# Four key weight tiles of the second block taken feature tile by feature tile, with two halves split before the normalisation root

## Chip, cores and metric

The kernel runs on one core of one Trainium2 chip, as one launch. The metric is the device time of that core in microseconds; of several runs the median counts. The engines are named as in the profile: PE is TensorE's matrix multiply and PEld its weight loads, DVE is VectorE, ACT is ScalarE, POOL is GpSimd, SP issues the weight stream's DMAs.

## What is computed

Three transformer-like blocks run over 256 tokens with 1024 features. The first two (`DEPTH = 2`) also carry 256 context tokens, so that their keys and values span 512 columns. The change lies at the seam between the first and the second block. There the reference does, for tokens `x` and context `xc`:

```python
x_new = x + gt[:, None] * rms_norm(out, norm_post[l])
...
h = rms_norm(x, norm_pre[l]) * (1.0 + sc[:, None]) + sh[:, None]
hc = rms_norm(xc, norm_pre[l]) * (1.0 + scc) + shc
z = h @ w_in[l]
zc = hc @ (w_in[l][:, :COL_Q] if last else w_in[l])
kc = qk_heads(zc[..., COL_K:COL_V])
...
k = apply_rope(qk_heads(z[..., COL_K:COL_V]), cos, sin)
```

The 512 key columns of `w_in` make four weight tiles, the 512 query columns four, the 512 value columns four. Keys are needed for all 512 columns (tokens and context), queries in the second block for the 256 tokens alone.

## The kernel before

Activations are kept feature-major: 1024 features are 8 feature tiles (`KT = 8`) of 128 partitions, with the 512 tokens along the free axis. Weights arrive as one stream of tiles of 128 x 1024 numbers (512 KB each), in the order in which they are used. Each tile `t` passes through four stations:

- SP loads it into one of `RAW = 4` slots; it waits until the slot's earlier tile has been split (`tile_lo`, t - 4).
- ACT writes the high half, rounded to fp32r (`act_hi`, L999, name `whi`). It waits for the landing and for `used`, t - 4: PE must be through with the tile whose `whi` slot is overwritten, since there are `SPLIT = 4` slots.
- DVE writes the low half, raw minus high (`dve_lo`, L1435, name `wlo`).
- PE multiplies it with three matmuls for each feature tile (`three`, L376 to L378: low by high, high by low, high by high), accumulating over the 8 feature tiles in one of four PSUM banks `gemm_bank`. The last matmul marks `used`, and ACT evacuates the bank (L1023 for key and query tiles).

Every engine works through a program written by hand, in order; a wait holds all that stands behind it. ACT has the high halves three tiles ahead of the tile it evacuates and DVE the low halves two tiles ahead.

Around the seam (`l = 1`) the program is as follows. PE sums the squares of the new `x`, turns two adaLN rows into columns (L519) and multiplies four adaLN tiles (L447). ACT splits the high halves of key tiles 0, 1 and 2, copies the adaLN row (L1018) and takes the root of the mean square (`act_root`, L990). DVE splits the low halves of key tiles 0 and 1, copies the turned adaLN values (L1550), finishes the modulation vectors (L1789, L1790), takes the reciprocal of the root (`dve_rstd`, L1427), and then makes the normalised input for each feature tile (`dve_h`): a sum on DVE (L1807, name `tmp`), the high half on ACT (L1233, name `hhi`), the low half on DVE (L1818, name `hlo`). PE's first key tile waits for each feature tile in turn (`begun`), the other three do not need to.

After `dve_h` DVE splits four tiles (key tiles 2 and 3, query tiles 0 and 1), then works out the argument of the third block's rotary cosine (`dve_trig`, L1635 to L1564, a long chain of small operations each of which waits for the one before), splits query tile 2, works out the argument of the sine, and then splits query tile 3 and three value tiles. ACT answers each argument with a `Sin` (L1266), ahead of which an ACT_TABLE_LOAD stands. DVE's second argument waits for ACT's first `Sin`, since both use one buffer; DVE's splitting of query tile 3 waits for the second.

Of the kernel before, what the change touches and what calls it, by code (L numbers as in the profile page):

```python
# [14 lines left out]
P = 128  # L15
D = 1024
KT = D // P
# [8 lines left out]
SPLIT = 4  # L26
# [20 lines left out]
          [("rope", P, ALL), ("perm1", P, P), ("inv_freq", P, 1), ("head_gain", P, 15), ("causal", P, P), ("cmp_add", P, 2 * NCMP),  # L47
           ("cmp_any", P, 2), ("perm2", P, P), ("head_sum", P, 14 * 32), ("block_mean", P, P), ("pe_k", P, 16), ("pe_v", P, 16),
           ("g_mix", P, 8), ("g_ffn", P, 8), ("g_ple", P, 8)]


def pi_parts():
# [152 lines left out]
class Kernel:  # L205
# [396 lines left out]
    def pe_front(self):  # L602
# [21 lines left out]
        self.pe_tiles(4)  # L624
        self.pe_turn(0, 3)

    def pe_first(self):

        self.pe_tiles(1)
        self.pe_taps(0)  # L630
        self.pe_tiles(4)
        self.pe_tap_norm(0)
        self.pe_tiles(2)
        self.pe_spec(0)
        self.pe_tiles(1)
# [148 lines left out]
    def pe_block1(self, l):  # L784
        n = TOK if l else ALL
        if l == 0:
            self.pe_first()
        self.pe_tiles(9 if l else 1)
        for a, b in ROPE:
            self.pe_rope(l, a, b)  # L790
            self.pe_tiles(1)
        if l == 0:
            self.pe_tiles(1)
        self.pe_attention(l)
        self.pe_conv(l)
        self.pe_tiles(4 if l else 1)
        self.pe_gmlp(l)
        self.pe_tiles(8 + (28 if l else 36))
        for o in range(KT):
            self.pe_tiles(1)  # L800
            if o:
                self.pe_sum(("out", l), o - 1, n)
            if l == 0 and o in (0, 2):
                self.pe_hidden(1, o // 2)
            if l == 0 and o == 4:
                self.pe_taps(1)
        if l == 0:
            self.pe.wait_ge(*self.at("taps", 1))
        self.pe_sum(("out", l), KT - 1, n)
        if l == 0:  # L810
            self.pe_tap_norm(1)
            self.pe_tiles(4)
            self.pe_spec(1)
        self.pe.wait_ge(*self.at("rstd", ("out", l)))
        for k in range(KT):
            self.pe_sum(("res", l), k, n)
        if l == 0:
            self.pe_turn(1, 4)
            self.pe_tiles(4)
            self.pe_turn(1, 5)  # L820
# [435 lines left out]
    def act_block1(self, l):  # L1256
        act, n = self.act, TOK if l else ALL
        if l:
            self.act_root(("res", 0), ALL)
        act.wait_ge(*self.at("mod", l))  # L1260
        self.act_h(l)
        if l:
            self.act_tiles(4)
            for i in range(2):
                act.wait_ge(*self.at("trig_arg", i))
                act.activation((self.cos, self.sin)[i], self.tmp[:, 1, 0:TOK], ACT.Sin).then_inc(*self.mark("act_filter", "trig", i))  # L1266
                if i == 0:
                    self.act_tiles(1)
            self.act_tiles(7)
        else:  # L1270
            self.act_first()
            self.act_tiles(4)
        if l == 0:
            self.act_tiles(1)
        self.act_attention(l)
        self.act_conv(l)
        self.act_tiles(4 if l else 1)
        self.act_gmlp(l)
        act.wait_ge(*self.at("gm_y", l, 1 if l else 3))
        self.act_tiles(8 + (28 if l else 36))  # L1280
        act.wait_ge(*self.at("evac", self.tiles[self.act_done - 1].use))
        self.act_merged(l, KT - 1, n)
        for o in range(KT):
            self.act_tiles(1)
            if l == 0 and o in (1, 3):
                self.act_hidden(1, o // 2)
            if l == 0 and o == 6:
                self.act_tap_sq(1)
        self.act_root(("out", l), n)
        if l == 0:  # L1290
            self.act_tap_root(1)
            self.act_tiles(4)
        for k in range(KT):
            act.wait_ge(*self.at("x_new", l, k))
            self.act_sq(("res", l), k, n, self.x[:, k, 0:n]).then_inc(*self.mark("act_sq", "sq", ("res", l), k))
            if l == 0 and k >= 3 and k < 7:
                self.act_kern(1, k - 3)
        if l == 0:
            self.act_tiles(4)
# [536 lines left out]
    def dve_block1(self, l):  # L1836
        v, n = self.dve, TOK if l else ALL
        if l:
            self.dve_rstd(("res", 0), ALL)
        self.dve_h(l)  # L1840
        if l:
            self.dve_tiles(4)
            self.dve_trig()
            self.dve_tiles(4)
        else:
            self.dve_first()
            self.dve_tiles(4)
        for a, b in ROPE:
            self.dve_rope(l, a, b)
            self.dve_tiles(1)  # L1850
        if l == 0:
            self.dve_tiles(1)
        self.dve_attention(l)
        self.dve_conv(l)
        self.dve_tiles(4 if l else 1)
        self.dve_gmlp(l)
        self.dve_tiles(8 + (28 if l else 36))
        self.dve_merged(l, KT - 1, n)
        for o in range(KT):
            self.dve_tiles(1)  # L1860
            if l == 0 and o in (0, 2):
                self.dve_hidden(1, o // 2)
            if l == 0 and o == 5:
                self.dve_taps(1)
                self.dve_tap_sd(1)
        if l == 0:
            self.dve_mod(1)
            self.dve_tap_add(1)
            self.dve_tiles(4)
        self.dve_rstd(("out", l), n)  # L1870
        if l == 0:
            self.dve_tap_rs(1)
        for k in range(KT):
            out = self.branch_out[:, k, 0:n]
            self.own(v.tensor_tensor(out, out, self.tmp[:, 2, 0:n], ALU.mult))
            v.tensor_tensor(self.x[:, k, 0:n], self.x[:, k, 0:n], out, ALU.add).then_inc(*self.mark("dve_x", "x_new", l, k))
        if l == 0:
            self.dve_turned(1, 4)
            self.dve_tiles(4)
            self.dve_turned(1, 5)  # L1880
            self.dve_mod_gate(1)
# [435 lines left out]
```

## Time and profile before

| what | value |
|---|---|
| median of 3 runs | 1585.3 us (1583.09 to 1588.12) |
| the profiled execution, its own time | 1588.17 us |
| its span in the profile | 1586.8 us |
| mean granted TensorE clock | 0.973 |
| PE busy | 1484.6 us, 94% of the span |
| DVE busy | 896.8 us, 57% |
| ACT busy | 675.2 us, 43% |
| the seam read here | 700 to 760 us of the span |

The profiled execution took 1.4 us more than its span, which is what lies outside of the instructions. It was 2.9 us slower than the median of the three timed runs, and equal to their highest. Times in the rows below are counted from the span's start. The busy share is an average over the whole kernel; the stretch of the change is read by itself.

### The profile page before, as it was taken

The numbers are of one execution on the slowest core, as the hardware profiler recorded it, in microseconds if no ns is written. First come the engines' busy times: TensorE is split into PE (matmuls) and PEld (weight loads), VectorE is DVE, ScalarE is ACT, GpSimd is POOL, SyncE is SP. The second block draws the span as 40 slices with busy tenths as digits, with TensorE's granted clock in tenths as the row PEclk, the third lists the DMA queues.
The fourth block names the chain that finished last, engine by engine and source line by source line (L and its number), as shares of the span: only waits on it lengthen the run. The fifth ranks groups of instructions, "written<-read, shape, count | busy, mean of one in ns | idle before, by whom it ended". The sixth has DMA issues, their size and how long they took to land. (4 is left out here: it accounts for less than half of the span.)

```text
span 1586.8 us, 22164 instructions
## 1 busy us (share of the span) xinstructions
PE 1484.6 (94%) x8986; PEld 1250.4 (79%) x8986; DVE 896.8 (57%) x1653; ACT 675.2 (43%) x1176; POOL 32.5 (2%) x42
## 2 busy tenths in 40 slices
PE   6799999987999999978989999988999999999998
PEld 2577667765888888736778889987878889999997
DVE  3525764654533434457576576656666547666546
ACT  3432544123322223444455354456556544544434
POOL 0000000000000000100000000010000001000000
PEclk9899999998999999999999999999999999999999
DMA  8521442124232322332323346544542215555552
GB/s 318 173 67 53 135 159 92 53 86 146 93 107 91 103 85 93 99 133 67 107 93 128 145 146 190 180 148 136 173 146 81 67 62 170 182 185 181 192 174 80
DMA packets 57847, 203.14 MB, mean 128 GB/s; under 512 B 6257, under 2 KB 9457, under 8 KB 57617
## 3 DMA queue, kind: packets, MB, share of 16 engines
q1 hardware_dynamic: 55568, 194.01, 37.0%
q0 software_dynamic: 1888, 7.12, 1.3%
q8 instruction: 71, 1.16, 0.3%
q10 hardware_dynamic: 288, 0.58, 0.1%
q14 instruction: 32, 0.25, 0.1%
HBM read 200.65 MB, written 1.05 MB: 127 GB/s over the span
## 5 line engine op out<-in xcount | busy, mean ns | idle before, releaser
L376 PE MATMUL gemm_bank<-hhi,wlo 128*128 128x256 f32 (+1 forms) x1264 | 415.5, 329 | 38.8 <-DVE wlo L1435 15.7
L1435 DVE TENSOR_TENSOR wlo<-raw,whi 128x1024 fp32r<-128x1024 f32 x316 | 381.0, 1219 | 75.7 <-ACT whi L999 71.7
L999 ACT ACTIVATE whi<-raw 128x1024 fp32r<-128x1024 f32 x316 | 332.0, 1052 | 189.3 <-PE gemm_bank L378 120.9
L377 PE MATMUL gemm_bank<-hlo,whi 128*128 128x256 f32 (+1 forms) x1264 | 399.0, 316 | 0.0
L378 PE MATMUL gemm_bank<-hhi,whi 128*128 128x256 f32 (+1 forms) x1264 | 398.2, 315 | 0.0
L376 PEld LDWEIGHTS gemm_bank<-hhi,wlo 128*128 128x128 f32 x1264 | 246.2, 195 | 67.3 <-issue 24.6
L378 PEld LDWEIGHTS gemm_bank<-hhi,whi 128*128 128x128 f32 x1264 | 246.5, 195 | 14.1
L377 PEld LDWEIGHTS gemm_bank<-hlo,whi 128*128 128x128 f32 x1264 | 247.2, 196 | 12.9 <-issue 0.7
L376 PE MATMUL misc_bank<-hhi,wlo 128*128 128x256 f32 (+1 forms) x496 | 160.7, 324 | 0.0
L377 PE MATMUL misc_bank<-hlo,whi 128*128 128x256 f32 (+1 forms) x496 | 160.7, 324 | 0.0
L378 PE MATMUL misc_bank<-hhi,whi 128*128 128x256 f32 (+1 forms) x496 | 160.7, 324 | 0.0
L376 PE MATMUL gemm_bank<-arena_r,wlo 128*128 128x256 f32 (+1 forms) x408 | 132.9, 326 | 0.6 <-issue 0.6
L378 PE MATMUL gemm_bank<-arena_r,whi 128*128 128x256 f32 (+1 forms) x408 | 132.5, 325 | 0.0
L377 PE MATMUL gemm_bank<-arena_r,whi 128*128 128x256 f32 (+1 forms) x408 | 132.5, 325 | 0.0
L376 PEld LDWEIGHTS misc_bank<-hhi,wlo 128*128 128x128 f32 x496 | 94.4, 190 | 7.5
L378 PEld LDWEIGHTS misc_bank<-hhi,whi 128*128 128x128 f32 x496 | 94.4, 190 | 7.5
L377 PEld LDWEIGHTS misc_bank<-hlo,whi 128*128 128x128 f32 x496 | 94.4, 190 | 7.4
L376 PEld LDWEIGHTS gemm_bank<-arena_r,wlo 128*128 128x128 f32 x408 | 77.6, 190 | 8.5 <-issue 2.3
L378 PEld LDWEIGHTS gemm_bank<-arena_r,whi 128*128 128x128 f32 x408 | 77.6, 190 | 6.3
L377 PEld LDWEIGHTS gemm_bank<-arena_r,whi 128*128 128x128 f32 x408 | 77.6, 190 | 6.1
L1470 DVE SCALAR_TENSOR_TENSOR tmp<-tmp,gemm_bank 128x512 f32<-128x512 f32 (+1 forms) x32 | 17.7, 555 | 104.1 <-ACT tmp L1060 104.1
L1060 ACT ACTIVATE tmp<-misc_bank 128x512 f32<-128x512 f32 (+1 forms) x40 | 20.5, 512 | 122.5 <-PE misc_bank L378 122.5
(334 smaller groups left out, 1942.4 us busy)
## 6 DMA issues: line engine op xcount, KB each, us to landing
raw<-in_stream SPq DMA_DIRECT2D x364, 512.0 KB, 3.5
const_b<-in_const_b POOLq DMA_DIRECT2D x1, 1100.0 KB, 8.7
x<-in_x SPq DMA_DIRECT2D x1, 1024.0 KB, 8.7
x<-in_ctx SPq DMA_DIRECT2D x1, 1024.0 KB, 11.0
y<-in_hy_decay POOLq DMA_DIRECT2D x2, 512.0 KB, 6.6
arena<-in_gm_ws POOLq DMA_DIRECT2D x2, 512.0 KB, 6.1
y<-in_hy_w POOLq DMA_DIRECT2D x2, 256.0 KB, 5.4
shared<-in_dft POOLq DMA_DIRECT2D x1, 512.0 KB, 4.1
```

What stands on the lines that cost most here:

```text
L376: mm(out, w_lo, r_hi, start=first, stop=False)
L377: mm(out, w_hi, r_lo, start=False, stop=False)
L378: return mm(out, w_hi, r_hi, start=False, stop=last)
L999: act.activation(self.whi[:, t % SPLIT, :], self.raw[:, t % RAW, :], ACT.Copy).then_inc(*self.mark("tile_hi", "tile_hi", t))
L1060: act.activation(self.tmp[:, e % 2, 0:n], self.M[e][:, 0:n], ACT.Tanh, scale=0.5).then_inc(*self.mark("act_sel", "sel_tanh", T.use))
L1435: dve.tensor_tensor(self.wlo[:, t % SPLIT, :], self.raw[:, t % RAW, :], self.whi[:, t % SPLIT, :].bitcast(F32), ALU.subtract).then_inc(*se ...
L1470: self.own(dve.scalar_tensor_tensor(th, th, 1.0, b[:, 0:n], ALU.add, ALU.mult))
```

## The change

Three things change, all in the second block, and no instruction is added or removed.

PE takes the four key tiles together (`pe_quad`, order in `QUAD`): (0, 1) means key tile 0, feature tile 1. Each of the four accumulates in its own bank. Up to feature tile 3 the tiles advance together, then tiles 0 and 1 in turns, then tile 2 and tile 3 to their ends. Key tiles 2 and 3 therefore need both their halves before PE begins with them, so ACT splits key tile 3 ahead of `act_root`, and DVE splits key tiles 2 and 3 ahead of `dve_rstd`. Behind `dve_h` as many splits are left out (`split=False`).

```diff
--- before.py
+++ after.py
@@ -47,6 +47,9 @@
           [("rope", P, ALL), ("perm1", P, P), ("inv_freq", P, 1), ("head_gain", P, 15), ("causal", P, P), ("cmp_add", P, 2 * NCMP),
            ("cmp_any", P, 2), ("perm2", P, P), ("head_sum", P, 14 * 32), ("block_mean", P, P), ("pe_k", P, 16), ("pe_v", P, 16),
            ("g_mix", P, 8), ("g_ffn", P, 8), ("g_ple", P, 8)]
+
+QUAD = [(0, 0), (0, 1), (1, 0), (1, 1), (0, 2), (1, 2), (2, 0), (2, 1), (2, 2), (0, 3), (1, 3), (2, 3), (3, 0), (3, 1), (3, 2), (3, 3)] + \
+       [(i, k) for k in range(4, KT) for i in (0, 1)] + [(i, k) for i in (2, 3) for k in range(4, KT)]
 
 
 def pi_parts():
@@ -624,6 +627,23 @@
         self.pe_tiles(4)
         self.pe_turn(0, 3)
 
+    def pe_quad(self):
+
+        pe, tiles, n = self.pe, self.tiles[self.pe_next:self.pe_next + 4], 0
+        for i, k in QUAD:
+            T = tiles[i]
+            s, c = T.t % SPLIT, slice(k * P, (k + 1) * P)
+            if k == 0:
+                pe.wait_ge(*self.at("tile_lo", T.t))
+                self.pe_bank(T.use)
+            if k == n:
+                pe.wait_ge(*self.at("h", T.l, k))
+                n += 1
+            m = self.three(self.G[T.use % 4][:, 0:T.n], self.whi[:, s, c], self.wlo[:, s, c], self.hhi[:, k, 0:T.n], self.hlo[:, k, 0:T.n], k == 0, k == KT - 1)
+            if k == KT - 1:
+                m.then_inc(*self.mark("tile_used", "used", T.t))
+                self.pe_next += 1
+
     def pe_first(self):
 
         self.pe_tiles(1)
@@ -785,7 +805,9 @@
         n = TOK if l else ALL
         if l == 0:
             self.pe_first()
-        self.pe_tiles(9 if l else 1)
+        if l:
+            self.pe_quad()
+        self.pe_tiles(5 if l else 1)
         for a, b in ROPE:
             self.pe_rope(l, a, b)
             self.pe_tiles(1)
@@ -1256,11 +1278,13 @@
     def act_block1(self, l):
         act, n = self.act, TOK if l else ALL
         if l:
+            self.act_hi()
             self.act_root(("res", 0), ALL)
         act.wait_ge(*self.at("mod", l))
         self.act_h(l)
         if l:
-            self.act_tiles(4)
+            self.act_tiles(1, split=False)
+            self.act_tiles(3)
             for i in range(2):
                 act.wait_ge(*self.at("trig_arg", i))
                 act.activation((self.cos, self.sin)[i], self.tmp[:, 1, 0:TOK], ACT.Sin).then_inc(*self.mark("act_filter", "trig", i))
@@ -1836,10 +1860,13 @@
     def dve_block1(self, l):
         v, n = self.dve, TOK if l else ALL
         if l:
+            for _ in range(2):
+                self.dve_lo()
             self.dve_rstd(("res", 0), ALL)
         self.dve_h(l)
         if l:
-            self.dve_tiles(4)
+            self.dve_tiles(2, split=False)
+            self.dve_tiles(2)
             self.dve_trig()
             self.dve_tiles(4)
         else:
```

The orders below are those of the built programs; names are as above, and in the changed kernel the lines are numbered 22 to 24 higher behind `pe_quad` and 3 higher ahead of it.

DVE at the seam, from the copy of the turned adaLN values to the first low half of the input, before:

```order
491 L1550 COPY mod<-gemm_bank 128x8 [waits pe_turn]
492 L1789 TENSOR_TENSOR mod<-mod,const_a 128x16 [waits dve_evac]
493 L1790 TENSOR_TENSOR mod<-mod,const_a 128x16 [waits dve_own]
494 L1427 RECIPROCAL tmp<-tmp 128x512 [waits act_root]
495 L1807 SCALAR_TENSOR_TENSOR tmp<-x,modA,tmp 128x256 [waits dve_mod,dve_rstd]
496 L1807 SCALAR_TENSOR_TENSOR tmp<-x,modA,tmp 128x256 x3
497 L1818 SCALAR_TENSOR_TENSOR hlo<-tmp,mod,hhi 128x256 [waits act_half]
```

and in the changed kernel:

```order
491 L1574 COPY mod<-gemm_bank 128x8 [waits pe_turn]
492 L1813 TENSOR_TENSOR mod<-mod,const_a 128x16 [waits dve_evac]
493 L1814 TENSOR_TENSOR mod<-mod,const_a 128x16 [waits dve_own]
494 L1459 TENSOR_TENSOR wlo<-raw,whi 128x1024 [waits tile_hi] x2
495 L1451 RECIPROCAL tmp<-tmp 128x512 [waits act_root]
496 L1831 SCALAR_TENSOR_TENSOR tmp<-x,modA,tmp 128x256 [waits dve_mod,dve_rstd]
497 L1831 SCALAR_TENSOR_TENSOR tmp<-x,modA,tmp 128x256 x3
```

Two low halves now stand between the modulation vectors and the reciprocal, and with them everything that `dve_h` issues.

ACT at the same place and at the first key evacuation (rows 337 to 351 are the other high halves of the input, 352 the high half of key tile 3), before:

```order
334 L1018 ACTIVATE const_a<-gemm_bank 128x512 [waits pe_turn,tile_used]
335 L990 ACTIVATE tmp<-misc_bank,const_a 128x512 [waits pe_sum]
336 L1233 ACTIVATE hhi<-tmp,mod 128x256 [waits dve_h,dve_mod]
...
352 L999 ACTIVATE whi<-raw 128x1024 [waits tile_used,raw3]
353 L1023 ACTIVATE arena<-gemm_bank 128x512 [waits tile_used]
354 L999 ACTIVATE whi<-raw 128x1024 [waits tile_used,raw0]
```

and in the changed kernel:

```order
334 L1040 ACTIVATE const_a<-gemm_bank 128x512 [waits pe_turn,tile_used]
335 L1021 ACTIVATE whi<-raw 128x1024 [waits tile_used,raw3]
336 L1012 ACTIVATE tmp<-misc_bank,const_a 128x512 [waits pe_sum]
337 L1255 ACTIVATE hhi<-tmp,mod 128x256 [waits dve_h,dve_mod]
...
353 L1045 ACTIVATE arena<-gemm_bank 128x512 [waits tile_used]
354 L1021 ACTIVATE whi<-raw 128x1024 [waits tile_used,raw0]
```

The high half of key tile 3 stands ahead of the root. The high half of query tile 0 (the last row of each) still follows the first key evacuation, and both wait for PE to be through with key tile 0.

PE at the key tiles, the first of the three matmuls of each step (the two others follow it with the same bank), before:

```order
2404 L376 MATMUL gemm_bank1<-hhi,wlo 128x512 [waits dve_half,act_evac,tile_lo]
...
2407 L376 MATMUL gemm_bank1<-hhi,wlo 128x512 [waits dve_half]
...
2425 L376 MATMUL gemm_bank1<-hhi,wlo 128x512 [waits dve_half]
...
2428 L376 MATMUL gemm_bank2<-hhi,wlo 128x512 [waits dve_evac,tile_lo]
...
2452 L376 MATMUL gemm_bank3<-hhi,wlo 128x512 [waits act_evac,tile_lo]
...
2476 L376 MATMUL gemm_bank0<-hhi,wlo 128x512 [waits dve_evac,tile_lo]
```

and in the changed kernel, where gemm_bank1, 2, 3 and 0 hold key tiles 0, 1, 2 and 3:

```order
2404 L379 MATMUL gemm_bank1<-hhi,wlo 128x512 [waits dve_half,act_evac,tile_lo]
...
2407 L379 MATMUL gemm_bank1<-hhi,wlo 128x512 [waits dve_half]
...
2410 L379 MATMUL gemm_bank2<-hhi,wlo 128x512 [waits dve_evac,tile_lo]
...
2416 L379 MATMUL gemm_bank1<-hhi,wlo 128x512 [waits dve_half]
...
2422 L379 MATMUL gemm_bank3<-hhi,wlo 128x512 [waits act_evac,tile_lo]
...
2431 L379 MATMUL gemm_bank1<-hhi,wlo 128x512 [waits dve_half]
...
2440 L379 MATMUL gemm_bank0<-hhi,wlo 128x512 [waits dve_evac,tile_lo]
...
2470 L379 MATMUL gemm_bank1<-hhi,wlo 128x512 [waits dve_half]
...
2473 L379 MATMUL gemm_bank2<-hhi,wlo 128x512
...
2476 L379 MATMUL gemm_bank3<-hhi,wlo 128x512
```

Before, key tile 0 is complete with the eighth step and each further tile with another eight; now key tile 0 is complete with step 23 of 32, key tile 1 with 24, key tile 2 with 28 and key tile 3 with 32.

## Rows read from the trace of the kernel before

**Rows 1.** Page, part 1: busy time, share of the span and instructions of each engine.

```profile
PE 1484.6 (94%) x8986; PEld 1250.4 (79%) x8986; DVE 896.8 (57%) x1653; ACT 675.2 (43%) x1176; POOL 32.5 (2%) x42
```

**Rows 2.** Stage windows, TensorE: stretch, its length, busy time (instructions), granted clock, DMA share, GB/s.

```profile
707.00:717.00 10.00, 1.84 (x8) 0.50 0.34 120
...
721.00:745.00 24.00, 21.43 (x90) 1.00 0.28 88
...
756.00:760.00 4.00, 3.43 (x26) 1.00 0.72 197
```

**Rows 3.** Timeline of VectorE, 710 to 729 us: start, duration, line, operation, tiles, [idle, releaser].

```profile
710.55 0.17 DVE L1550 COPY mod<-gemm_bank 128x8 f32<-128x8 f32 x1 [2.63 <-PE gemm_bank L519]
...
711.06 3.35 DVE L1427 RECIPROCAL tmp<-tmp 128x512 f32<-128x512 f32 x1
...
716.35 0.88 DVE L1818 SCALAR_TENSOR_TENSOR hlo<-tmp,mod,hhi 128x256 fp32r<-128x256 f32 x2 [0.24 <-ACT hhi L1233]
...
727.72 2.35 DVE L1435 TENSOR_TENSOR wlo<-raw,whi 128x1024 fp32r<-128x1024 f32 x2
```

**Rows 4.** Timeline of TensorE over the key tiles, in the same columns.

```profile
717.38 0.77 PE L376 MATMUL gemm_bank<-hhi,wlo 128*128 128x512 f32 x1 [6.86 <-DVE hlo L1818]
...
720.46 0.50 PE L376 MATMUL gemm_bank<-hhi,wlo 128*128 128x512 f32 x1
...
722.04 0.50 PE L376 MATMUL gemm_bank<-hhi,wlo 128*128 128x512 f32 x1 [0.62 <-DVE hlo L1818]
...
728.66 0.40 PE L376 MATMUL gemm_bank<-hhi,wlo 128*128 128x512 f32 x1
...
745.00 0.28 PE L376 MATMUL gemm_bank<-hhi,wlo 128*128 128x256 f32 x1
```

**Rows 5.** Timeline of ScalarE from the third key tile to the first key evacuation.

```profile
706.99 1.06 ACT L999 ACTIVATE whi<-raw 128x1024 fp32r<-128x1024 f32 x1 [0.33 <-DMA raw<-in_stream]
...
708.43 0.68 ACT L990 ACTIVATE tmp<-misc_bank,const_a 128x512 f32<-128x512 f32 x1
...
728.86 0.60 ACT L1023 ACTIVATE arena<-gemm_bank 128x512 f32<-128x512 f32 x1 [1.02 <-PE gemm_bank L378]
729.35 1.05 ACT L999 ACTIVATE whi<-raw 128x1024 fp32r<-128x1024 f32 x1
```

**Rows 6.** Timeline of VectorE, 730 to 760 us.

```profile
730.43 1.23 DVE L1435 TENSOR_TENSOR wlo<-raw,whi 128x1024 fp32r<-128x1024 f32 x1 [0.36 <-ACT whi L999]
735.89 1.23 DVE L1435 TENSOR_TENSOR wlo<-raw,whi 128x1024 fp32r<-128x1024 f32 x1 [4.24 <-ACT whi L999]
737.04 0.29 DVE L1635 CAST tmp<-pos 128x256 f32<-128x256 int32 x1
...
743.93 1.22 DVE L1435 TENSOR_TENSOR wlo<-raw,whi 128x1024 fp32r<-128x1024 f32 x1
747.56 0.29 DVE L1635 CAST tmp<-pos 128x256 f32<-128x256 int32 x1 [2.41 <-ACT x L1266]
...
754.70 4.63 DVE L1435 TENSOR_TENSOR wlo<-raw,whi 128x1024 fp32r<-128x1024 f32 x4 [0.48 <-ACT x L1266]
```

**Rows 7.** Timelines near 787 us: a table load on ScalarE, then VectorE.

```profile
787.38 1.28 ACT L1168 ACT_TABLE_LOAD   x1
...
787.69 0.17 DVE L1656 TENSOR_SCALAR stat<-stat 128x2 f32<-128x2 f32 x1
```

**Rows 8.** Timeline of TensorE at the last query tile and the first value tile.

```profile
755.98 0.39 PE L376 MATMUL gemm_bank<-hhi,wlo 128*128 128x256 f32 x1 [2.19 <-DVE wlo L1435]
...
759.68 0.47 PE L376 MATMUL gemm_bank<-whi,hlo 128*128 128x512 f32 x1 [0.57 <-ACT arena L1023]
```

**Rows 9.** Stage windows of TensorE around two other idle stretches.

```profile
343.00:348.00 5.00, 0.29 (x6) 1.00 0.59 210
348.00:352.00 4.00, 3.26 (x8) 0.57 0.38 131
...
386.00:393.00 7.00, 6.95 (x21) 0.52 0.61 210
```

## Prediction

> **What bounds the kernel now.** I read the page first, then the windows of the seam, then one engine's timeline after the other in the order in which they wait. PE is busy for 94% of the span [rows 1], so almost every microsecond by which PE's own chain moves at one place moves the end. The seam is an exception to the 94%: from 707 to 717 us PE works for 1.84 of 10 us and its granted clock falls to 0.50, which is the 1.2 GHz level; from 721 on it is at 1.00, 2.4 GHz [rows 2]. What PE waits for is DVE's chain: the reciprocal starts at 711.06, right behind the modulation vectors that follow the copy at 710.55, the first low half of the input starts at 716.35 [rows 3], and PE's first key matmul starts at 717.38 after 6.86 us of idle [rows 4]. From there PE is fed feature tile by feature tile: three tiles in 722.04 - 717.38 = 4.66 us, 1.55 us each, and at 722.04 it sat idle for 0.62 us for the next [rows 4]. From 728.66 it runs free: 24 steps of three matmuls in 745.00 - 728.66 = 16.34 us, 0.681 us a step [rows 4]. The reader should also see the second wait at this seam. DVE is in the long rotary chain (from 737.04) and splits query tile 3 only at 754.70 [rows 6]; PE sat idle 2.19 us for it and started at 755.98 [rows 8]. So two DVE chains end the waits here, not PE's matmuls between them. Behind it PE has one more wait of 0.57 us for an evacuation that hangs on PE's own work [rows 8].
>
> **What the change does to the start.** Two low halves move ahead of the reciprocal. Before, the pair takes 2.35 us behind the input [rows 3]; what follows a split starts some 0.08 us before its end (737.04 behind 735.89 + 1.23 [rows 6]), so the reciprocal and all of `dve_h` slip by 2.27 us. Nothing covers this: DVE's idle time (2.63 us, up to 710.55 [rows 3]) lies ahead of the copy, and the two halves stand behind it in an in-order program. Both high halves they wait for are there: key tile 2's ends at 708.05, and key tile 3's takes the root's place at 708.43 and ends at 709.5 [rows 5]; its load follows the three before it, which came 1.3 us or so apart, and I take it as landed by then. ACT's root moves from 708.43 by 1.06 us and ends near 710.2 [rows 5], 3.1 us ahead of the reciprocal's new start at 713.33, so this edit costs nothing; uncovered it would cost 1.06. The earlier freeing of two raw slots lets SP ask for two query tiles sooner; ACT takes them only once PE frees `whi` slots, so nothing comes of it. PE starts at 717.38 + 2.27 = 719.65.
>
> **What it gives back on PE.** The first two steps took 720.46 - 717.38 = 3.08 us, mostly at the low clock [rows 2, 4]. Taking the same, PE is at 722.73 with 30 steps to go, and now has work of other tiles in the gaps of 0.62 us: a new feature tile arrives every 1.55 us, the last by 730.5, and is first needed at steps 5, 10 and 17 and then every second one, from 724.1 on, 727.5 and 732.3, so it is always there. 30 x 0.681 = 20.43 us: the key tiles end at 743.2, against 745.00 [rows 4], 1.8 us earlier in spite of the late start. A clock that rises a step or so later costs up to 0.75 us of this.
>
> **What is late next.** Key tile 0 is now done after step 23, at 722.73 + 21 x 0.681 = 737.0, where before it was done with step 8 at 728.66. Before, ACT evacuated at 728.86 (0.2 us behind the end) and began query tile 0's high half at 729.35, for 1.05 us [rows 5]; DVE split it at 730.43 [rows 6]. Now: evacuation 737.2, high half 737.7 to 738.8, next evacuation, high half of query tile 1 from 739.2 to 740.3 (key tile 1 is done at 737.7, no wait), low half at 740.3. Before it was at 735.89 [rows 6]: 4.4 us late. The rotary argument stands right behind it: 737.04 becomes 741.45. The argument takes 743.93 - 737.04 = 6.89 us [rows 6], so query tile 2 is split at 748.34 instead of 743.93. Here 2.4 us come back: the second argument waited 2.41 us for ACT's `Sin` [rows 6], which stood behind key tile 3's evacuation and a table load. Now that evacuation ends near 744.0 and the load is through by 745.3, as a load doesn't wait for the operand: another one starts at 787.38 while DVE's last operation ahead of its activation starts only at 787.69 [rows 7]. So the second argument starts when the split is issued, at 748.34 + 1.15 = 749.5, against 747.56 [rows 6]: 1.95 us late. Query tile 3 is split at 754.70 + 1.95 = 756.65 [rows 6], and PE takes it at 755.98 + 1.95 = 757.9 [rows 8]. Queued behind it on PE is the whole rest of the block, which before was driven by PE. If the table load did wait, 0.8 us more.
>
> PE's gain turns into idle time: query tiles take (755.98 - 2.19 - 745.00) / 3 = 2.93 us each [rows 4, 8]. PE starts them at 743.2, waits for the third until 749.6, ends it at 752.6 and sits idle for 5.4 us.
>
> **What the idle time does to the clock.** Elsewhere PE worked for only 0.29 of 5 us (343 to 348), and in the 4 us that follow the mean clock is 0.57 [rows 9]: (1 - 0.57) / 0.5 x 4 = 3.4 us at the low level. In the 7 us from 386 it is 0.52: 6.7 us low [rows 9]. At the seam the 2.19 us wait left it high, at 1.00 from 756 to 760 [rows 2]. 5.4 us is like the first. PE loses half of the time that it works at the low level: none (bound below), 1.7 us (3.4 us wholly in work), 3.4 us (6.7 us). I take 1.5, since part of the first spell fell in idle time. The Trainium skill (TensorE: Matmul & The Clock Gate, Why this matters for your kernels) advises against idle gaps between bursts of matmuls, because the clock then falls back; it speaks against this change, and by that rule, with which this trace agrees, the time is 1588.8, and without it 1587.3.
>
> **Sum.** +1.95 (the later second argument) + 1.5 (clock) = +3.5 us. The profiled execution was 1588.17 us, so it would be 1591.7; the median of three was 1585.3, and to that the same sum gives 1588.8. That is 0.22%.
>
> One price is disputed. A 512-column matmul started 0.681 / 3 = 0.227 us after the one before [rows 4]. The Trainium skill (TensorE: Matmul & The Clock Gate, Back-to-back issue gap) gives about 131 ns for a stream of load and multiply pairs at that width. By it a step would be 0.393 us, the second argument would start 4.1 us earlier than before, and the time would be near 1581.2; this trace has 24 steps that say otherwise, and the sum keeps to them.
>
> **The rivals.**
> - *The clock stays high* through the 5.4 us: +1.95, 1587.3. For it: the 2.19 us wait did no harm; against: rows 9. Chance 0.20.
> - *The low clock lasts 6.7 us*: +1.95 + 3.4 = +5.3, 1590.6, slower by over 0.3% (4.8 us). It decides from 5.7 us of work at the low level on. Rows 9 have one spell of this length and one of 3.4. Chance 0.13.
> - *Faster: the sine chain is not what PE waits for*, so that the 1.8 us of the key tiles reach the end: 1583.5. It needs query tile 3 split at 752.9 or sooner, 3.8 us ahead of what I find; for it speaks only that PE's wait there is short now, 2.19 us. Chance 0.09.
> - *The two splits cost the start nothing*, the change not being later at all there: then all of the above up to the arguments is 2.27 us sooner, query tile 2 is split at 746.06, the second argument starts at 747.2, 0.35 before 747.56 [rows 6], and with the clock's 1.5 it is +1.15, 1586.4. DVE's fixed order is against it. Chance 0.08.
> - *The forecast*, +3.5, 1588.8, between +2.4 and +5: chance 0.50.
>
> **How the numbers follow.** The range leaves out the faster case and the far ends: 1584.0 to 1591.5; it holds the forecast, the high clock, the long low clock and a start that is not delayed, and about 1 us on each side for a median of few runs, whose three values before were 5 us apart. About 0.3% is what a measurement of this kernel can tell from no change. Slower by more: the long low clock less a quarter (0.10) and a fifth of the forecast's cases (0.10): 0.20. Faster by more: a third of the faster case, 0.03. Within: 0.77.
>
> **What would show each step.** In the changed profile: the two splits stand from about 711.1 to 713.4 and the reciprocal after them (right or wrong for the start); PE's first key matmul at 719.7 and almost no idle time until 743.2 (the give-back); the first key evacuation at 737.2; the rotary chain from 741.5, its second part from 749.5; one idle stretch of PE above 5 us for a low half, ending at 757.9, and a granted clock of 0.50 just behind it. I am wrong if the first query tile's low half comes before 735, if the second part starts before 748, or if a wait of some microseconds that exists in both kernels behind 760 us swallows the shift: then the time would be unchanged.

## The result and the profile after

The changed kernel takes 1591.88 us, the median of 14 runs (1589.13 to 1594.87); the kernel before, run beside it, 1587.19 us, also of 14 (1583.09 to 1589.61). The ratio is 1.0026, with a 95% interval of 1.0017 to 1.0035: slower by 4.1 us (2.7 to 5.6), within the 0.3% that the prediction called no measurable change, and clear of zero. (The two medians themselves lie 4.7 us apart, inside that interval.)

The page of the profiled execution (its own time was 1591.25 us), span and part 1:

```profile
span 1589.9 us, 22164 instructions
...
PE 1485.1 (93%) x8986; PEld 1254.2 (79%) x8986; DVE 896.3 (56%) x1653; ACT 675.0 (42%) x1176; POOL 32.5 (2%) x42
```

PE's busy time is 1485.1 us against 1484.6 [rows 1]. It did the same work, and its share fell because it waited longer. The seam shows where. It can be cut out by two instructions that both kernels have: DVE's second copy of turned adaLN values (710.55 in [rows 3]) and PE's first matmul of a value tile (759.68 in [rows 8]). Stage windows of the kernel before, cut there; the columns are stretch, length, then busy time and instructions of PE, PEld, DVE, ACT and POOL, granted clock, DMA share, GB/s:

```profile
0.00:710.55 710.55, 660.72 (x2924) 490.79 (x2924) 337.89 (x552) 247.19 (x391) 14.54 (x22) 0.97 0.34 116
710.55:759.68 49.13, 36.97 (x192) 29.82 (x193) 39.62 (x80) 20.58 (x36) 0.00 (x0) 0.90 0.23 73
759.68:1586.00 826.32, 786.89 (x5870) 729.74 (x5870) 519.25 (x1021) 407.44 (x750) 17.96 (x20) 0.98 0.44 142
```

and of the changed kernel:

```profile
0.00:707.20 707.20, 658.05 (x2924) 489.30 (x2924) 337.71 (x552) 248.05 (x392) 14.52 (x22) 0.97 0.34 117
707.20:759.90 52.70, 37.40 (x193) 32.23 (x193) 39.54 (x80) 19.53 (x35) 0.00 (x0) 0.84 0.24 74
759.90:1589.90 830.00, 789.70 (x5870) 732.64 (x5870) 519.05 (x1021) 407.44 (x750) 17.96 (x20) 0.98 0.43 140
```

The seam took 49.1 us and takes 52.7, 3.6 us more at a mean clock of 0.84 instead of 0.90. The two other stretches hold the same instructions in both kernels (but for key tile 3's high half on ACT, which now stands ahead of the copy: 392 for 391), and yet they differ by -3.4 and +2.9 us between these two executions (the last one to the end of the span: 1586.8 - 759.68 = 827.1 against 830.0). I take that as the scatter of single executions: the changed kernel and four kernels below have the same program up to the copy, and their copies start anywhere from 706.95 to 710.71. This is the reason why below the seam of each trace stands beside the ratio of the timed runs.

DVE's timeline in the changed kernel:

```profile
707.20 0.17 DVE L1574 COPY mod<-gemm_bank 128x8 f32<-128x8 f32 x1 [3.14 <-PE gemm_bank L522]
...
707.71 2.35 DVE L1459 TENSOR_TENSOR wlo<-raw,whi 128x1024 fp32r<-128x1024 f32 x2
709.98 3.34 DVE L1451 RECIPROCAL tmp<-tmp 128x512 f32<-128x512 f32 x1
...
737.30 1.22 DVE L1459 TENSOR_TENSOR wlo<-raw,whi 128x1024 fp32r<-128x1024 f32 x1 [0.20 <-ACT whi L1021]
738.45 0.28 DVE L1659 CAST tmp<-pos 128x256 f32<-128x256 int32 x1
...
746.48 0.29 DVE L1659 CAST tmp<-pos 128x256 f32<-128x256 int32 x1
...
753.61 4.63 DVE L1459 TENSOR_TENSOR wlo<-raw,whi 128x1024 fp32r<-128x1024 f32 x4 [0.48 <-ACT x L1290]
```

The two low halves stand at 707.71, ahead of the reciprocal at 709.98: 709.98 - 707.20 = 2.78 us behind the copy, where it was 711.06 - 710.55 = 0.51 [rows 3]. The start is late by 2.27 us. The rotary argument starts 31.25 us behind the copy, before 26.49; the second one 39.28, before 37.01 [rows 6]. Neither has an idle bracket: the second no longer waits for ACT.

ACT's timeline:

```profile
705.08 1.05 ACT L1021 ACTIVATE whi<-raw 128x1024 fp32r<-128x1024 f32 x1
706.03 0.68 ACT L1012 ACTIVATE tmp<-misc_bank,const_a 128x512 f32<-128x512 f32 x1
...
734.29 0.60 ACT L1045 ACTIVATE arena<-gemm_bank 128x512 f32<-128x512 f32 x1 [8.48 <-PE gemm_bank L381]
...
741.03 1.28 ACT L1290 ACT_TABLE_LOAD   x1
745.46 0.42 ACT L1290 ACTIVATE x<-tmp 128x256 f32<-128x256 f32 x1 [3.15 <-DVE tmp L1588]
```

The high half of key tile 3 is at 705.08 and the root behind it ends at 706.71, over 3 us ahead of the reciprocal, which does not wait for it. The first key evacuation comes only at 734.29. The table load at 741.03 is done at 742.31 and the activation behind it starts at 745.46, 3.15 us later: here the load did not wait for the activation's operand.

PE's timeline:

```profile
716.30 0.76 PE L379 MATMUL gemm_bank<-hhi,wlo 128*128 128x512 f32 x1 [9.13 <-DVE hlo L1842]
...
740.21 0.28 PE L379 MATMUL gemm_bank<-hhi,wlo 128*128 128x256 f32 x1
...
746.62 0.39 PE L379 MATMUL gemm_bank<-hhi,wlo 128*128 128x256 f32 x1 [0.49 <-DVE wlo L1459]
...
754.89 0.58 PE L379 MATMUL gemm_bank<-hhi,wlo 128*128 128x256 f32 x1 [5.15 <-DVE wlo L1459]
...
759.90 0.47 PE L379 MATMUL gemm_bank<-whi,hlo 128*128 128x512 f32 x1 [0.56 <-ACT arena L1045]
```

The key tiles run from 716.30 to 740.21, 23.9 us instead of 27.6 [rows 4], without an idle bracket. Their end is 33.0 us behind the copy and was 34.5. Then the third query tile waits for 0.49 us and the last for 5.15. The stage windows of PE around that wait (length, busy time, granted clock):

```profile
750.00:754.80 4.80, 0.00 (x0) 0.97 0.00 0
754.90:757.80 2.90, 2.90 (x13) 0.50 0.65 189
758.00:762.00 4.00, 3.44 (x21) 1.00 0.89 306
```

PE does nothing for 4.8 us (a mean of 0.97 in that window means that the clock fell near 754.5, while PE still stood idle), then runs the last query tile at 0.50, the 1.2 GHz level, and is back at 1.00 from 758 on.

### The profile page after: what moved, and what is told of

Same layout as the page of the kernel before. It is cut to its first block and busy times, and to the rows that moved or that the text cites. A ratio compares the mean times of both kernels' runs of the same rounds, so it can differ in the third digit from the quotient of the medians.

```text
span 1589.9 us, 22164 instructions
## 1 busy us (share of the span) xinstructions
PE 1485.1 (93%) x8986; PEld 1254.2 (79%) x8986; DVE 896.3 (56%) x1653; ACT 675.0 (42%) x1176; POOL 32.5 (2%) x42
```

## Experiments

All kernels were timed in five rounds beside the kernel before. "Seam" is the time from the second adaLN copy on DVE to PE's first value-tile matmul in the profiled execution. A shift of 1.6 us is 0.1% of the time.

**Splits alone.** The key tiles go back to one after the other; the splits stay ahead of the root.

```diff
-        if l:
-            self.pe_quad()
-        self.pe_tiles(5 if l else 1)
+        self.pe_tiles(9 if l else 1)
```

> The splits stay ahead of the root, the key tiles go back to one after the other. The seam is measured from VectorE's second copy of turned adaLN values to TensorE's first value-tile matmul: 49.1 us before, 52.7 us in the changed kernel. Theory (two splits delay the start, late key tiles delay the sine chain, the idle time costs clock): only the start's 2.3 us remain, so 51.4 us, ratio 1.0014, an idle stretch of 2.2 us ahead of the last query tile and the clock high behind it. Rival 1 (the interleaving alone makes the loss, the splits hide): 49.1 us, 1.000. Rival 2 (the splits alone make the loss): 52.7 us, 1.0026.

Ratio 1.0017 (1.0005 to 1.0028). The copy on DVE, then PE's last query tile and first value tile:

```profile
706.95 0.17 DVE L1572 COPY mod<-gemm_bank 128x8 f32<-128x8 f32 x1 [3.54 <-PE gemm_bank L522]
...
754.64 0.39 PE L379 MATMUL gemm_bank<-hhi,wlo 128*128 128x256 f32 x1 [2.18 <-DVE wlo L1457]
...
758.34 0.47 PE L379 MATMUL gemm_bank<-whi,hlo 128*128 128x512 f32 x1 [0.56 <-ACT arena L1043]
```

Seam 51.4 us, as expected: the late start alone, 2.3 us, passes through to the end, with the idle stretch of 2.18 us as in the kernel before. Both rivals fall in the trace: the splits are not hidden, and they are not the whole loss. The ratio alone settles only the first: its interval, up to 1.0028, still holds the second rival's 1.0026.

**Four tiles together, splits in DVE's idle time.** They move from behind the modulation vectors to ahead of the second copy, where DVE waited.

```diff
-            for _ in range(2):
-                self.dve_lo()
             self.dve_rstd(("res", 0), ALL)
...
             self.dve_turned(1, 4)
             self.dve_tiles(4)
+            for _ in range(2):
+                self.dve_lo()
             self.dve_turned(1, 5)
```

> The changed kernel with the two low halves of key tiles 2 and 3 moved from behind the modulation vectors to ahead of the second copy, into VectorE's idle time. Theory: the start is no longer late, but the key tiles are still released late; second argument 0.35 us earlier than before, copy 0.2 us later, clock 1.3 us lost: seam 50.3 us, ratio 1.0007, and an idle stretch near 5 us ahead of the last query tile. Rival (the splits alone make the loss and TensorE's 1.8 us of saved work then reach the end): 47.3 us, 0.9989 or lower. Rival (no effect of the place): 52.7 us.

Ratio 1.0014 (1.0002 to 1.0026). DVE's copy and its second argument, PE's last query tile and first value tile, and the window of PE between those two:

```profile
710.70 0.16 DVE L1574 COPY mod<-gemm_bank 128x8 f32<-128x8 f32 x1
...
747.31 0.29 DVE L1659 CAST tmp<-pos 128x256 f32<-128x256 int32 x1
...
755.72 0.58 PE L379 MATMUL gemm_bank<-hhi,wlo 128*128 128x256 f32 x1 [5.14 <-DVE wlo L1459]
...
761.77 0.48 PE L379 MATMUL gemm_bank<-whi,hlo 128*128 128x512 f32 x1 [0.56 <-ACT arena L1045]
...
755.70:761.70 6.00, 5.49 (x24) 0.50 0.79 246
```

PE starts as early as before, and the second argument is 36.6 us behind the copy (before 37.0, changed 39.3): 0.4 us early, as worked out. Yet PE still sits idle for 5.14 us, since the last query tile's half follows the second argument, and the clock was low for the whole 6 us behind it in this execution. Seam 51.1 us, of which the clock is more than I gave it: the last query and the step to the first value tile took 761.77 - 755.72 = 6.05 us, 3.70 at the high clock [rows 8]. That is the 6.7 us spell of the rivals, seen once. The seam is counted from the copy and so leaves out 0.1 us by which the splits push the copy itself back (PE was done with the turn at 710.56). In this execution PE's interleaved work gained nothing, even from an early start: the last query tile came 0.4 us earlier and the clock cost 2.35.

**Idle time filled, ten matmuls.** The changed kernel, with extra matmuls of constants whose result nobody reads.

```diff
             self.pe_quad()
-        self.pe_tiles(5 if l else 1)
+            self.pe_tiles(3)
+            for _ in range(10):
+                self.pe.matmul(self.M[3][:, :], self.c["mean_all"], self.c["rope"], start=True, stop=True)
+        self.pe_tiles(2 if l else 1)
```

> The changed kernel with ten extra matmuls of constants into a free bank, ahead of the last query tile, in TensorE's idle time of 5.2 us; their result is not used. Theory: the granted clock stays at 1.00 through the last query tile, the seam is 1.3 us shorter than the changed kernel's: 51.4 us, ratio 1.0014 or so. Rival (the clock is not what the last query tile loses to): 52.7 us, 1.0026.

Ratio 1.0039 (1.0025 to 1.0053). PE's timeline at the extra matmuls (a matmul of 4-byte floats shows as two instructions) and the window behind them:

```profile
752.92 8.75 PE L812 MATMUL misc_bank<-const_b,const_a 128*128 128x512 f32 x20
...
761.70:764.00 2.30, 2.30 (x21) 1.00 0.87 328
```

They took 8.75 us where I had counted on about 5, so the last query tile started 50.6 us behind the copy instead of 47.7 (seam 54.6 us). The clock stayed at 1.00, but the expectation of the time missed, by my sizing, and the run decides nothing on it. Hence the next.

**Idle time filled, five matmuls.** `range(5)` in place of `range(10)`.

> As the one with ten extra matmuls, but with five: ten took 8.75 us, longer than the idle time, and pushed the last query tile back; five take 4.4 us and fit into 5.2. Seam (second adaLN copy to first value-tile matmul; 49.1 us before, 52.7 changed). Theory (the low clock costs the last query tile 1.3 us): clock 1.00 through that tile, the tile still starts 47.7 us behind the copy, seam 51.4 us, ratio 1.0014. Rival (something else slows it): seam 52.7 us though the clock is high, ratio 1.0026.

Ratio 1.0008 (0.9998 to 1.0019). DVE's copy, PE's last query and first value tile, and the window of the query tile:

```profile
710.60 0.17 DVE L1577 COPY mod<-gemm_bank 128x8 f32<-128x8 f32 x1 [3.34 <-PE gemm_bank L522]
...
758.19 0.39 PE L379 MATMUL gemm_bank<-hhi,wlo 128*128 128x256 f32 x1 [0.84 <-DVE wlo L1462]
...
761.89 0.47 PE L379 MATMUL gemm_bank<-whi,hlo 128*128 128x512 f32 x1 [0.56 <-ACT arena L1048]
...
758.20:761.00 2.80, 2.80 (x23) 1.00 0.60 186
```

The last query tile starts 47.6 us behind the copy (47.7 in the changed kernel), but at a clock of 1.00, and takes 3.70 us to the first value tile instead of 5.01. Seam 51.3 us. So 1.3 to 1.4 us of the changed kernel's loss in the traced executions are the clock's, by adding work and removing none. By the ratios it is 1.0026 - 1.0008, or 2.9 us, twice as much. The two intervals just overlap (1.0017 and 1.0019), so this settles nothing, but the low clock may well cost the timed executions more than it cost the traced one.

**Two tiles together, no split moved.** From the kernel before:

```diff
+    def pe_pair(self):
+        pe, tiles = self.pe, self.tiles[self.pe_next:self.pe_next + 2]
+        for k in range(KT):
+            for i, T in enumerate(tiles):
...
+                if i == 0:
+                    pe.wait_ge(*self.at("h", T.l, k))
+                m = self.three(self.G[T.use % 4][:, 0:T.n], self.whi[:, s, c], self.wlo[:, s, c], self.hhi[:, k, 0:T.n], self.hlo[:, k, 0:T.n], k == 0, k == KT - 1)
...
-        self.pe_tiles(9 if l else 1)
+        if l:
+            self.pe_pair()
+        self.pe_tiles(7 if l else 1)
```

> The kernel before with only key tiles 0 and 1 interleaved, feature tile by feature tile, and no split moved ahead. Theory: the start is not delayed, both tiles are done near 18 us after the copy where before only one was, the rotary argument starts 3 us earlier, the second one is then held by the table load behind key tile 3's evacuation and starts 4.1 us earlier: seam 45.0 us, ratio 0.9974. Rival (alternating banks costs TensorE something, or the sine chain is not what decides): 47 us or more, 0.999 to 1.000.

Ratio 0.9978 (0.9968 to 0.9988), faster. DVE's copy and second argument, PE's last query and first value tile, and the window of PE between those two:

```profile
711.24 0.17 DVE L1568 COPY mod<-gemm_bank 128x8 f32<-128x8 f32 x1 [3.38 <-PE gemm_bank L519]
...
745.27 0.29 DVE L1653 CAST tmp<-pos 128x256 f32<-128x256 int32 x1 [1.65 <-ACT x L1284]
...
753.69 0.39 PE L376 MATMUL gemm_bank<-hhi,wlo 128*128 128x256 f32 x1 [2.18 <-DVE wlo L1453]
...
758.90 0.47 PE L376 MATMUL gemm_bank<-whi,hlo 128*128 128x512 f32 x1 [0.56 <-ACT arena L1041]
...
753.70:758.00 4.30, 4.30 (x24) 0.61 0.67 201
```

Seam 47.7 us, not 45.0. The second argument still waits for ACT (1.65 us) and starts 34.0 us behind the copy, 3.0 early and not 4.1: the clock at the start rose 2.8 us later than I had assumed (12.7 us behind the copy; it was 9.9 before), which moves key tile 3 and the table load behind it. The rest is the low clock behind an idle stretch of only 2.18 us, which cost 1.5 us. The ratio is better than this seam alone would give (1.5 / 1588, 0.9991), so I take it that many of the timed executions don't meet that low clock; no trace shows them. The direction is settled by the ratio, and the size by it alone.

**First argument early, four tiles together.** In the changed kernel DVE takes the first rotary argument right behind the input, ACT its `Sin`, and the second argument comes behind query tiles 0 and 1.

```diff
             self.dve_tiles(2, split=False)
-            self.dve_tiles(2)
             self.dve_trig()
-            self.dve_tiles(4)
+            self.dve_tiles(5)
...
             if i == 0:
-                self.dve_tiles(1)
+                self.dve_tiles(2)
             v.wait_ge(*self.at("trig", i))
...
-            self.act_tiles(1, split=False)
-            self.act_tiles(3)
             for i in range(2):
...
                 if i == 0:
-                    self.act_tiles(1)
+                    self.act_tiles(1, split=False)
+                    self.act_tiles(4)
             self.act_tiles(7)
```

> The changed kernel with VectorE's first rotary argument moved into its 9 us of idle time right behind the input, ScalarE's Sin with it, and the second argument behind the splits of query tiles 0 and 1. Theory (the sine chain decides when TensorE gets the last query tiles): the start is still 2.3 us late, but no idle stretch above 1.5 us remains and no low clock behind it; seam 46.7 us, 2.4 us less than before and 6 less than the changed kernel, ratio 0.9985. Rival (TensorE's interleaved steps are the loss): seam 52 us or more, 1.002.

Ratio 0.9985 (0.9975 to 0.9996). DVE's copy and second argument, the longest wait of PE behind it and PE's first value tile:

```profile
710.71 0.17 DVE L1573 COPY mod<-gemm_bank 128x8 f32<-128x8 f32 x1 [2.95 <-PE gemm_bank L522]
...
741.80 0.29 DVE L1658 CAST tmp<-pos 128x256 f32<-128x256 int32 x1
...
750.22 0.39 PE L379 MATMUL gemm_bank<-hhi,wlo 128*128 128x256 f32 x1 [0.74 <-DVE wlo L1458]
...
756.80 0.47 PE L379 MATMUL gemm_bank<-whi,hlo 128*128 128x512 f32 x1 [0.56 <-ACT arena L1045]
```

Seam 46.1 us, 0.6 less than expected, and 0.74 us is the longest wait left behind the start. The late start and the interleaving are as in the changed kernel; taking the sine chain from behind the key tiles turned a loss of 3.6 us into a gain of 3.0. The rival falls.

**The same with the splits in DVE's idle time.**

> The same with the two splits also moved ahead of the second copy, so that both delays are gone. Theory: the two mends add up: 2.3 us less again, seam 44.4 us, ratio 0.9970. Rival (they overlap, the splits' place matters only while the sine chain is late): as without it, 46.7 us, 0.9985.

Ratio 0.9974 (0.9963 to 0.9985). DVE's copy, PE's first value tile and a window of PE at the start of the key tiles:

```profile
707.81 0.16 DVE L1573 COPY mod<-gemm_bank 128x8 f32<-128x8 f32 x1
...
752.74 0.47 PE L379 MATMUL gemm_bank<-whi,hlo 128*128 128x512 f32 x1 [0.56 <-ACT arena L1045]
...
714.60:720.60 6.00, 5.97 (x14) 0.50 0.00 0
```

Seam 44.9 us: 1.2 us less, not 2.3. PE started 2.3 us earlier behind the copy (6.8 instead of 9.1), but this time the clock rose 12.9 us behind it, as in the run before (12.8), so that 6.1 us were spent at the low level instead of 3.7, at a cost of half the difference, 1.2. In the traces the mends add up less what the clock takes back; the two intervals overlap, so only the trace tells them apart.

**First argument early, two tiles together.** The pair, with DVE's order: key tiles 2 and 3 split, first argument, four query tiles split, second argument.

```diff
-            self.dve_tiles(4)
+            self.dve_tiles(2)
             self.dve_trig()
-            self.dve_tiles(4)
+            self.dve_tiles(3)
...
             if i == 0:
-                self.dve_tiles(1)
+                self.dve_tiles(4)
             v.wait_ge(*self.at("trig", i))
...
-            self.act_tiles(4)
+            self.act_tiles(2)
             for i in range(2):
...
                 if i == 0:
-                    self.act_tiles(1)
-            self.act_tiles(7)
+                    self.act_tiles(4)
+            self.act_tiles(6)
```

> The kernel before with key tiles 0 and 1 interleaved (seam 47.7 us by itself, where the second argument still came too late by 2.2 us of idle time and a low clock followed), and the first rotary argument moved ahead of the splits of the query tiles. Theory: TensorE never waits more than 1 us behind the input, seam 44.0 us, ratio 0.9968. Rival (the pair has already taken what there is): 47.7 us, 0.9978.

Median 1582.12 us of 5 runs against 1587.96 of 29; ratio 0.9964 (0.9950 to 0.9977). DVE's copy, PE's first value tile and a window of PE in the key tiles:

```profile
708.57 0.17 DVE L1568 COPY mod<-gemm_bank 128x8 f32<-128x8 f32 x1 [2.60 <-PE gemm_bank L519]
...
751.52 0.47 PE L376 MATMUL gemm_bank<-whi,hlo 128*128 128x512 f32 x1 [0.94 <-ACT arena L1041]
...
719.00:724.00 5.00, 5.00 (x24) 1.00 0.00 0
```

Seam 43.0 us, 6.2 less than before and 9.7 less than the changed kernel. It beats both. It is also 1.0 us less than expected, and that is the clock's doing: it rose 10.3 us behind the copy here, 12.7 in the run with two tiles alone, and the key tiles end 30.3 us behind it instead of 31.5. For the same reason its lead of 1.9 us over the run before this one is not shown to be more than the clock (12.9 there, key tiles done at 31.7); the intervals of the two overlap.

**First argument early, nothing else.** The last diff without the pair.

> The kernel before with its key tiles one after the other, and only the first rotary argument moved ahead of the splits of the query tiles. Theory (the sine chain is a bound by itself, in the kernel before too): the 2.2 us of idle time ahead of the last query tile go, key tiles as before, seam (second adaLN copy to first value-tile matmul) 46.9 us against 49.1 us, ratio 0.9986. Rival (the chain matters only once the key tiles are interleaved): 49.1 us, 1.000.

Ratio 0.9980 (0.9971 to 0.9989). DVE's copy and PE's first value tile:

```profile
705.96 0.17 DVE L1550 COPY mod<-gemm_bank 128x8 f32<-128x8 f32 x1 [3.17 <-PE gemm_bank L519]
...
753.00 0.47 PE L376 MATMUL gemm_bank<-whi,hlo 128*128 128x512 f32 x1 [0.94 <-ACT arena L1023]
```

Seam 47.0 us, 2.1 less. The sine chain was a bound in the kernel before too, by nearly all of the 2.19 us of [rows 8].

The ten comparisons beside one another; "by the seam" is 1 + (seam - 49.1) / 1588:

| kernel | seam, us | by the seam | measured ratio |
|---|---|---|---|
| changed | 52.7 | 1.0023 | 1.0026 |
| splits alone | 51.4 | 1.0014 | 1.0017 |
| four tiles, splits in idle time | 51.1 | 1.0013 | 1.0014 |
| four tiles, filled with ten | 54.6 | 1.0035 | 1.0039 |
| four tiles, filled with five | 51.3 | 1.0014 | 1.0008 |
| two tiles | 47.7 | 0.9991 | 0.9978 |
| four tiles, argument early | 46.1 | 0.9981 | 0.9985 |
| the same, splits in idle time | 44.9 | 0.9974 | 0.9974 |
| two tiles, argument early | 43.0 | 0.9962 | 0.9964 |
| argument early | 47.0 | 0.9987 | 0.9980 |

Nine of ten seams lie within the interval of their ratio; two tiles alone do not, for the reason given there.

## Why the prediction was right

The forecast was +3.5 us, the measured ratio means +4.1 (2.7 to 5.6), and the trace's seam says +3.6. Point by point, counted from the copy on DVE (710.55 in the kernel before, so that a predicted 719.65 is 9.1):

- *The start.* Predicted 2.27 us late; the reciprocal is 2.27 late and PE's first key matmul is 9.1 behind the copy. Shown by the trace and by the splits alone, which cost 2.3 us. The ACT edit cost nothing.
- *What it gives back on PE.* Predicted the end of the key tiles at 32.6, found 33.0. The clock rose after 4.1 us of steps instead of 3.1 (13.2 us behind the copy, before 9.9), within the 0.75 us named for it.
- *What is late next.* Predicted the first argument at 30.9 and the second at 38.95, found 31.25 and 39.3: both 0.3 late, inherited from the clock. The 2.4 us that come back because the second argument no longer waits for ACT came back; without that the second argument would have been 4.7 us late. PE took the last query tile at 47.7 (predicted 47.4).
- *The idle stretch.* Predicted 5.4 us, found 5.15, behind 0.49 for the third query tile.
- *The clock.* Predicted 1.5 us; 1.3 by the step from the last query tile to the first value tile (5.01 against 3.70), 1.4 by the filled kernel (52.7 against 51.3). The spell lasted from 754.5 to 757.9, 3.4 us, with its first 0.4 in idle time. The advice of the Trainium skill (TensorE: Matmul & The Clock Gate, Why this matters for your kernels) against idle gaps held here, with 0.50 behind the 5.15 us. That the size came out is in part luck. The price was taken from one other stretch of the trace, chosen because its idle time was like the expected one. But the stretch of [rows 9] with the long spell has the shorter idle time, 4.23 us against 5.45 ahead of the key matmul at 348.74:

```profile
386.05 1.84 PE L519 MATMUL gemm_bank<-const_a 128*128 128x2 f32 x8 [4.23 <-ACT const_a L1018]
```

So the length of the idle time did not tell the two spells apart, and the sister kernel with the splits in idle time met the long one behind 5.14 us.

The two terms also missed in opposite directions: the later tile was 2.26 us and not 1.95, the clock 1.3 and not 1.5. That the sum is within 0.1 us of the trace's seam owes something to this.

The other side of the argument also held: the 1.5 us by which PE ends the key tiles sooner could not reach the end. With an early start and no other mend the four tiles together were still slower than before (1.0014). The rival that the clock stays low for 6.7 us was not the changed kernel's profiled execution, but it was that of its sister with the splits in idle time; how often it comes is not known. And 0.227 us a matmul was the right price: 32 steps took 23.9 us, while 96 matmuls at 0.131 us and 2.0 for the 4.0 us at the low clock would be 14.6. The 131 ns of the Trainium skill (TensorE: Matmul & The Clock Gate, Back-to-back issue gap) do not hold for this stream, which the trace shows at 0.227 us.

What the runs shown could not tell is the level. The changed kernel's own median, 1591.88 us, is 0.4 us above the range's upper end, because the median of three from which the sum went out, 1585.3, lies 1.9 us below that of fourteen. The ratio on 1585.3 us gives 1589.4, 0.6 above the forecast.

## What to carry to other kernels

Interleaving several accumulations fills the consumer's gaps, but it releases all of their buffers at the end: look for who waits for the first release (here a weight slot, then a split, then 14 us of small operations on another engine) before counting the filled gaps as gain. Work moved "ahead" on an in-order engine is free only if it stands ahead of the wait, not just behind it; here the place three instructions too late moved the start by 2.3 us. When a long chain on a side engine ends a wait, move that chain first: this alone gave 2.1 us in the trace, and two tiles together with it 6.2 (some 1 us of that by a clock that rose early), where four tiles without it lost 3.6. A single trace of a seam carries a microsecond or two of the clock's scatter, so set the timed ratio beside it.

## What the hardware showed that I had not expected

- Filling idle time with matmuls of no use shortened the seam: the changed kernel's fell from 52.7 to 51.3 us, because the next tile ran at a granted clock of 1.00 instead of 0.50.
- The same idle length has different outcomes. 2.2 us of idle time ahead of the last query tile left the clock at 1.00 in the kernel before and was followed by 0.61 over 4.3 us with two tiles together; 5.14 and 5.15 us were followed by 6 us at 0.50 in one kernel and by 2.9 us at 0.50 in the other.
- At the start of the key tiles the clock rose between 9.9 and 13.2 us behind the same copy, in different executions. Where tiles are interleaved this moves their end: four tiles with the early start ended 30.3 us behind the copy when the clock rose at 10.1, and 31.7 when it rose at 12.9. One after the other they ended 34.5 and 34.4 us behind it, with the clock rising at 9.9 (kernel before) or at 12.4 (argument early): PE then waits for each feature tile anyway, and the late rise costs nothing.
